# Down projections of a two-layer transformer kernel: eight of 22 combining sums a layer moved to accumulating DMA, LayerNorm rows behind the last weight halves

## The reference, cut to what matters

```python
def conv_ffn(x, w_up, conv_w, conv_b, w_down):
    up = x @ w_up
    a, g = up[..., :D_FF], up[..., D_FF:]
    g = causal_dwconv(g, conv_w) + conv_b
    return (jax.nn.gelu(g) * a) @ w_down

for layer in range(DEPTH):            # DEPTH = 2
    ...
    x = layer_norm(alpha * x + conv_ffn(x, ffn_w_up[layer], ffn_conv_w[layer],
                                        ffn_conv_b[layer], ffn_w_down[layer]),
                   ln_ffn_g[layer], ln_ffn_b[layer])
```

## Time and profile before

| | us |
|---|---|
| runs | 1760.81, 1761.2, 1763.09 |
| median | 1761.2 |
| the profiled execution's own time | 1760.65 |
| span of the profile | 1758.8 |
| TensorE busy / weight loads | 1728.8 / 1447.6 |
| VectorE, ScalarE, GpSimd busy | 1110.8, 684.7, 184.4 |

### The profile page before, as it was taken

The page is one execution under the profiler, slowest core; times in us unless marked ns, Lnnn a source line. Parts: engine busy times, 40 slices in busy tenths (PEclk is TensorE's granted clock), DMA queues, the critical chain, the costliest instruction groups (busy, mean ns, idle before and its releaser), DMA issues.

```text
span 1758.8 us, 27808 instructions
## 1 busy us (share of the span) xinstructions
PE 1728.8 (98%) x11461; PEld 1447.6 (82%) x11461; DVE 1110.8 (63%) x1624; ACT 684.7 (39%) x1045; POOL 184.4 (10%) x246
## 2 busy tenths in 40 slices
PE   8999999999999999999999999999998999999998
PEld 7888988988888879888998888888886767777766
DVE  5567266454568795454726755567988585566784
ACT  5332352232235643213235232223554543345452
POOL 4202001200011112000210200001112000011000
PEclk9999999999999999999999999999999999999999
DMA  9882912973345858833492265455683422112412
GB/s 301 259 217 99 252 39 79 279 230 110 126 138 186 260 166 204 247 97 118 114 283 77 83 204 156 143 183 185 201 277 108 153 65 81 34 43 62 169 37 84
DMA packets 175453, 270.44 MB, mean 154 GB/s; under 512 B 10488, under 2 KB 97780, under 8 KB 174560
## 3 DMA queue, kind: packets, MB, share of 16 engines
q1 hardware_dynamic: 147488, 189.90, 34.2%
q0 software_dynamic: 26368, 73.51, 15.7%
q10 hardware_dynamic: 1472, 5.26, 0.8%
HBM read 253.67 MB, written 61.09 MB: 179 GB/s over the span
## 4 chain that ended last, share of the span: by engine, by line
PE 88%; DVE 7%; issue 2%; ACT 1%; DMA 1%; POOL 1%; SPq 0%; ACTq 0%; DVEq 0%
PE ps L365 26%; PE ps L367 26%; PE ps L366 26%; DVE WL L342 2%; PE ps L1007 2%; PE ps L554 1%; PE ps L2575 1%; PE ps L2595 1%; PE ps L2589 1%; DMA RAW<-ffn_w_down 1%; PE ps L1981 0%; DVE SM L1637 0%; PE ps L2609 0%; DVE LATE L2656 0%; PE ps L2712 0%
## 5 line engine op out<-in xcount | busy, mean ns | idle before, releaser
L342 DVE TENSOR_TENSOR WL<-RAW,WH 128x1024 fp32r<-128x1024 f32 x325 | 393.3, 1222 | 387.7 <-ACT WH L332 387.2
L332 ACT ACTIVATE WH<-RAW 128x1024 fp32r<-128x1024 f32 x325 | 341.0, 1058 | 559.8 <-PE ps L367 450.6
L365 PE MATMUL ps<-XH,WH 128*128 128x512 f32 (+1 forms) x1416 | 524.6, 370 | 2.6 <-DVE WL L342 1.5
L367 PE MATMUL ps<-XH,WL 128*128 128x512 f32 (+1 forms) x1416 | 518.1, 366 | 0.0
L366 PE MATMUL ps<-XL,WH 128*128 128x512 f32 (+1 forms) x1416 | 517.9, 366 | 0.0
L365 PEld LDWEIGHTS ps<-XH,WH 128*128 128x128 f32 x1416 | 267.4, 189 | 50.1 <-issue 5.3
L367 PEld LDWEIGHTS ps<-XH,WL 128*128 128x128 f32 x1416 | 267.3, 189 | 43.3
L366 PEld LDWEIGHTS ps<-XL,WH 128*128 128x128 f32 x1416 | 267.5, 189 | 40.7
L365 PE MATMUL ps<-WH,XH 128*128 128x512 f32 x696 | 279.1, 401 | 7.9 <-DVE WL L342 7.0
L367 PE MATMUL ps<-WH,XL 128*128 128x512 f32 x696 | 271.9, 391 | 0.0
L366 PE MATMUL ps<-WL,XH 128*128 128x512 f32 x696 | 271.6, 390 | 0.0
(11 more groups left out here) (404 smaller groups left out, 2063.7 us busy)
## 6 DMA issues: line engine op xcount, KB each, us to landing
RAW<-ffn_w_up SPq DMA_DIRECT2D x176, 256.0 KB, 3.5
weight_sums<-ffn_w_down POOLq DMA_DIRECT2D x12, 1536.0 KB, 18.5
RAW<-w_in SPq DMA_DIRECT2D x33, 512.0 KB, 3.9
RAW<-xa_wkv SPq DMA_DIRECT2D x32, 512.0 KB, 7.5
RAW<-weight_sums SPq DMA_DIRECT2D x32, 512.0 KB, 4.6
weight_sums<-ffn_w_down POOLq DMA_DIRECT2D x12, 1280.0 KB, 31.1
RAW<-c_w_in SPq DMA_DIRECT2D x24, 512.0 KB, 7.2
LATE<-w_ada SPq DMA_DIRECT2D x24, 512.0 KB, 5.2
```

The source lines that it names most:

```text
L332: e.activation(halves_of(i)[0][:, :, 0:w], raw(i)[:, :, 0:w], ACT.Copy).then_inc(*w_hi.up(i))
L342: e.tensor_tensor(wl[:, :, 0:w], raw(i)[:, :, 0:w], wh[:, :, 0:w].bitcast(F), ALU.subtract).then_inc(*w_lo.up(i))
L365: e.matmul(o, lh, rh, start=start, stop=False)
L367: return e.matmul(o, ll, rh, start=False, stop=stop)
```

## The change

- ScalarE multiplies the residual by alpha in place, one row tile after each of the column blocks 2 to 5 of the up projection (`residual_act`).
- Eight of the 22 combining instructions become accumulating transfers that GpSimd issues (`combined_pool`): XR's blocks += U (rows 0, 1, column block 0), += the sum of U and product 6 (rows 2, 3, block 0), += Y (all rows, block 1). The sum no longer overwrites U but has its own place (`sum_place`). The adds and subtractions of product 7 move to steps 26 and 27; VectorE waits there, at step 28 and in rows 0 and 1 for the transfers.
- LayerNorm rows 0 and 1 move from steps 30 to 33 to behind the low half of chunk 39, ahead of rows 2 and 3; `row` is split in `row` and `row_g`, and the parts of neighbouring rows are interleaved.
- On TensorE, in layer 0, `behind(0)` moves from behind the last chunk of u = 0 to behind the second of the four chunks of u = 1, where `behind(1)` was, and `behind(1)` to behind all of e.
- On GpSimd `combined_pool` stands behind `down_pool`, ahead of `early_pool` and the LayerNorm steps.

```diff
@@ -316,6 +316,7 @@
     sum_in = {name: [sig(f"sum_{name}{g}", "dma", 16) for g in range(2)] for name in ("t1", "t2", "t3", "t4")}
     tok_out, tok_in = sig("tok_out", "dma", 16), [sig(f"tok_in{i}", "dma", 16) for i in range(3)]
     dn_a = sig("dn_a", "A")
+    comb = {name: sig(f"comb_{name}", "dma", 16) for name in ("x11", "x12", "x21", "x22")}
 
     made = {"hi": 0, "lo": 0, "w": 0}
 
@@ -1270,6 +1271,8 @@
             for i in range(2):
                 gate_act(e, l, nb, i)
                 gelu_act(e, l, nb, i)
+            if 2 <= nb < 6:
+                residual_act(e, l, turned, nb - 2)
         hi_to(e, first["up", l, 10] + 3 + NH)
         for i in range(2):
             gate_act(e, l, 10, i)
@@ -1277,6 +1280,11 @@
         hi_to(e, first["up", l, 10] + 4 + NH)
         gelu_act(e, l, 10, 0)
         gelu_act(e, l, 10, 1)
+
+    def residual_act(e, l, turned, t):
+        for q in range(2):
+            e.wait_ge(*turn.at((turned, t, q)))
+        e.activation(XR[:, t, :], XR[:, t, :], ACT.Copy, scale=ALPHA).then_inc(*ffn_a.up(("residual", l, t)))
 
     def gate_act(e, l, nb, i):
         j, key = 2 * nb + i, (("up", l, nb), 2 + i)
@@ -1351,6 +1359,27 @@
     U = [SCR[:, 1028 + 512 * u:1540 + 512 * u] for u in range(2)]
     Y = [SCR[:, 512 * u:512 * u + 512] for u in range(2)]
 
+    def sum_place(l, u):
+        return late(512 + 512 * u, 512) if l == 0 else late(4096 + 1024 * u, 512)
+
+    def combined_pool(e, l):
+        n = ("ffn", l)
+
+        def added(name, t, j, src):
+            e.wait_ge(*ffn_a.at(("residual", l, t)))
+            e.dma_start(XR[:, t, 512 * j:512 * j + 512], src, accum_op=ALU.add).then_inc(*comb[name].up((l, t)))
+        for u in range(2):
+            e.wait_ge(*dn_a.at(("u", l, u)))
+            added("x11", u, 0, U[u])
+        for u in range(2):
+            e.wait_ge(*ln_v.at((n, "sum", u)))
+            added("x21", 2 + u, 0, sum_place(l, u))
+        for u in range(2):
+            e.wait_ge(*ln_v.at((n, "y", u)))
+            added("x12", u, 1, Y[u])
+        for u in range(2):
+            added("x22", 2 + u, 1, Y[u])
+
     def token_place(l):
         return (late(1536, 512), late(2816, 256)) if l == 0 else (late(5120, 512), late(5632, 256))
 
@@ -1583,8 +1612,9 @@
             for u in range(2):
                 for q in range(2, 6):
                     part(name, q, u)
-                    if name == "e" and (u, q) in ((0, 5), (1, 3)):
-                        behind(u)
+                    if name == "e" and (u, q) == (1, 3):
+                        behind(0)
+        behind(1)
         ps.back(*[("down", l, p, u) for p in (3, 4) for u in range(2)])
 
     def items_at(s):
@@ -1636,9 +1666,6 @@
         def stats_of(t, j):
             e.bn_stats(stats[:, t, j, :], x(t, j)).then_inc(*ln_v.up((n, t, j, "stats")))
 
-        def scaled(t, j, src):
-            return e.scalar_tensor_tensor(out=x(t, j), in0=x(t, j), scalar=ALPHA, in1=src, op0=ALU.mult, op1=ALU.add)
-
         def add(p, t, j):
             key = ("down", l, p, t % 2)
             e.tensor_tensor(x(t, j), x(t, j), ps.tile(key)[:, :], ALU.add).then_inc(*ps.empties(key, ln_v, (n, t, j)))
@@ -1648,7 +1675,7 @@
             u = t % 2
             if t < 2:
                 e.wait_ge(*gemm.at(("down", l, 3, u)))
-                e.wait_ge(*ln_v.at((n, "x12", u)))
+                e.wait_ge(*comb["x12"].at((l, 1)))
                 add(3, t, 1)
                 stats_of(t, 1)
             else:
@@ -1656,6 +1683,8 @@
                 e.wait_ge(*ln_v.at((n, "x21", u)))
                 add(4, t, 0)
                 stats_of(t, 0)
+
+        def row_g(t):
             norm_g_dve(e, XR[:, t, :], n, t, 2, GB[:, 0:1024], gb_in.at(n))
 
         def row_end(t):
@@ -1665,49 +1694,35 @@
             item_lo(e, l, m)
         for s in range(34):
             for u in range(2):
-                if s == 20:
+                if s == 21:
                     e.wait_ge(*dn_a.at(("u", l, u)))
-                    scaled(u, 0, U[u]).then_inc(*ln_v.up((n, "x11", u)))
-                if s == 21:
                     e.wait_ge(*gemm.at(("down", l, 6, u)))
-                    e.wait_ge(*ln_v.at((n, "x11", u)))
-                    e.tensor_tensor(U[u], U[u], ps.tile(("down", l, 6, u))[:, :], ALU.add).then_inc(
+                    if l:
+                        e.wait_ge(*tok_out.at((l, 10)))
+                    e.tensor_tensor(sum_place(l, u), U[u], ps.tile(("down", l, 6, u))[:, :], ALU.add).then_inc(
                         *ps.empties(("down", l, 6, u), ln_v, (n, "sum", u)))
                 if s == 22:
                     e.wait_ge(*ln_v.at((n, "sum", u)))
                     e.wait_ge(*gemm.at(("down", l, 5, u)))
-                    e.tensor_tensor(Y[u], ps.tile(("down", l, 5, u))[:, :], U[u], ALU.subtract).then_inc(
+                    e.tensor_tensor(Y[u], ps.tile(("down", l, 5, u))[:, :], sum_place(l, u), ALU.subtract).then_inc(
                         *ps.empties(("down", l, 5, u), ln_v, (n, "y", u)))
-                if s == 23:
-                    e.wait_ge(*ln_v.at((n, "y", u)))
-                    scaled(u, 1, Y[u]).then_inc(*ln_v.up((n, "x12", u)))
-                if s == 24:
+                if s == 26:
                     e.wait_ge(*gemm.at(("down", l, 7, u)))
-                    scaled(2 + u, 0, ps.tile(("down", l, 7, u))[:, :]).then_inc(*ln_v.up((n, "ax21", u)))
-                if s == 25:
-                    scaled(2 + u, 1, Y[u]).then_inc(*ln_v.up((n, "ax22", u)))
-                if s == 26:
-                    e.wait_ge(*ln_v.at((n, "ax22", u)))
+                    e.wait_ge(*comb["x21"].at((l, 3)))
+                    e.tensor_tensor(x(2 + u, 0), x(2 + u, 0), ps.tile(("down", l, 7, u))[:, :], ALU.add).then_inc(
+                        *ln_v.up((n, "x21", u)))
+                if s == 27:
+                    e.wait_ge(*comb["x22"].at((l, 3)))
                     e.tensor_tensor(x(2 + u, 1), x(2 + u, 1), ps.tile(("down", l, 7, u))[:, :], ALU.subtract).then_inc(
                         *ps.empties(("down", l, 7, u), ln_v, (n, "x22", u)))
-                if s == 27:
-                    e.wait_ge(*ln_v.at((n, "ax21", u)))
-                    e.tensor_tensor(x(2 + u, 0), x(2 + u, 0), U[u], ALU.add).then_inc(*ln_v.up((n, "x21", u)))
                 if s == 28:
                     e.wait_ge(*gemm.at(("down", l, 2, u)))
+                    e.wait_ge(*comb["x11"].at((l, 1)))
                     add(2, u, 0)
                     stats_of(u, 0)
                 if s == 29:
                     e.wait_ge(*ln_v.at((n, "x22", u)))
                     stats_of(2 + u, 1)
-            if s == 30:
-                row(0)
-            if s == 31:
-                row_end(0)
-            if s == 32:
-                row(1)
-            if s == 33:
-                row_end(1)
             lo_to(e, min(i0 + s + 1 + NH, limit))
             if s == 1:
                 token_sums(e, l, 9)
@@ -1715,27 +1730,37 @@
                 token_sums(e, l, 10)
             for m in items_at(s):
                 item_lo(e, l, m)
+        lo_to(e, i0 + 35 + NH)
         if l:
-            lo_to(e, n_in2)
             e.wait_ge(*ada_v.at(("mod", 5)))
             e.scalar_tensor_tensor(out=s1, in0=mod[:, 8:16], scalar=1.0, in1=VEC[:, vcol["ng"]:vcol["ng"] + 8],
                                    op0=ALU.add, op1=ALU.mult).then_inc(*rms_v.up("s1"))
-            for t in range(2, 4):
+            for t in range(4):
                 row(t)
-                if t == 3:
-                    bias_dve(e, 2)
-                row_end(t)
+                if t:
+                    row_end(t - 1)
+                row_g(t)
+            bias_dve(e, 2)
+            row_end(3)
             bias_dve(e, 3)
             e.wait_ge(*rms_g.at(3))
             lo_to(e, n_in2 + 1)
             return
+        row(0)
+        row_g(0)
         lo_to(e, i0 + 36 + NH)
+        row_end(0)
+        row(1)
+        row_g(1)
         turn_dve(e, n, 0)
+        row_end(1)
         row(2)
+        row_g(2)
         turn_dve(e, n, 1)
         lo_to(e, i0 + 37 + NH)
         row_end(2)
         row(3)
+        row_g(3)
         lo_to(e, i0 + 38 + NH)
         row_end(3)
         lo_to(e, i0 + 39 + NH)
@@ -3122,6 +3147,7 @@
                         sums_pool(e, 1, 0)
                     tokens_pool(e, l)
                     down_pool(e, l)
+                    combined_pool(e, l)
                 if (name, l) == ("ffn", 1):
                     early_pool(e)
                 for t in range(4):
```

## The result

| | before | after |
|---|---|---|
| median (19 runs each) | 1761.73 us | 1766.1 us |
| lowest to highest | 1760.03 to 1765.18 | 1764.17 to 1769.8 |
| the profiled execution's own time / span | 1760.65 / 1758.8 | 1765.43 / 1763.4 |

The ratio is 1.0026, 95% interval 1.0019 to 1.0032: slower by a little more than the 0.2% that a measurement of this kernel can tell from no change. The forecast was 1764.0 in a range of 1757.5 to 1767.0. The time lies in it, 2.1 us above the forecast. The growth of 4.4 us is more than the 3.5 us that the prediction had called the same: that outcome had 0.62 there, and slower 0.25. The span grew by 4.6 us, where the sum had said 2.8. The question of this part is where the other 1.8 us are, and whether the terms of the sum are what the chip does or only happen to add up.

What follows compares the result with a forecast made beforehand. TensorE, busy 98% of the span, was taken as the bound. From a profiled 1760.65 us, +1.0 - 0.2 + 2.0 = +2.8 gives 1763.45; with the median 0.55 above it, 1764.0 us, range 1757.5 to 1767.

Steps and rivals of the forecast that it cites:

- The stalls: Four TensorE waits for low weight halves ending both down projections, 5.95 us, all go; gross gain 7.4 us.
- Layer 0, +1.0: At the next gemm's second chunk after layer 0, TensorE arrives 1.0 us later than before (0.3 to 2.0).
- the count: VectorE's work in layer 0 up to the next gemm's second chunk: 27.6 us, with waits 29.1, low half ready at 671.65.
- The three waits: In layer 0 TensorE waits at row 1's turn and the next gemm's first and second chunks, about 4.1 us.
- Layer 1, -0.2: Row 3's end in layer 1 starts at 1359.8 against 1359.96: -0.2 us (-0.8 to +1.0).
- Links: Steps from one row end to the next in layer 1, over VectorE, ScalarE and GpSimd: 4.6 us each, 5.0 before.
- The sign that was given: What would show the prediction right in layer 1: row 3's end within 1 us of 1359.96.
- The pause and the clock, +2.0: TensorE stands 4.9 us before layer 1's fifth transpose; the lower clock slows later transposes: +2.0 us (0 to 3.5).
- Rival B: Waits moved as forecast but TensorE's clock held through layer 1's pause: 1762.0 us, chance 0.25.
- What was costed at nothing: ScalarE's four scalings a layer and the eight transfers GpSimd issues cost nothing; the last transfer has 16 us of cover.
- Rival D: Accumulating transfers land late, VectorE waits at steps 26 and 27; 10 us beyond cover in one layer gives 1774, chance 0.07.
- Rival C: The removed stalls pay: layer 0 keeps 3.1 us and layer 1 some 3, giving 1755.1 us, chance 0.13.

Runs made afterwards that it cites:

- Rows alone: Experiment 2: kernel before with all 22 combining instructions, only the change's places of LayerNorm rows 0 and 1 and their turns, no transfers: 1764.4 us, ratio 1.0011.
- experiment 3: Changed kernel with the early transfers for the second block held until chunk 34 of layer 1's down projection instead of chunk 3: 1765.06 us, ratio 1.0012.
- experiment 4: Changed kernel with 40 more transposes, results unused, after row 0's fourth, filling TensorE's pause: 1765.3 us, ratio 1.0018.
- experiment 5: Rows alone with row 0's add, statistics and (x - mean) * g back at step 30, its end behind the last low half: 1761.65 us, ratio 1.0001.
- experiment 1: Changed kernel with rows 0 and 1 back at steps 30 to 33 and TensorE's turns at their old places: 1767.02 us, ratio 1.003.
- experiment 9: Experiment 5 with TensorE's turn of row 0 back after the sixth part of block e, as before the change: 1759.16 us, ratio 0.9976.
- experiment 8: Experiment 1 with the early transfers of the next stage held until chunk 34 instead of chunk 3: 1768.47 us, ratio 1.0042.

## Why the prediction was right, and what it missed

- **The stalls.** All four went; TensorE's first new wait is behind block e. Right.
- **Layer 0, +1.0.** Rows alone gave +1.19, +1.04 without the offset, with c1's low half ending 0.1 us from the 671.65 that the count gave (670.64 and 1.14 for it). The three waits were 3.2 us in all, where 4.1 were foretold. Right in place and size. The changed kernel has +1.88. Without the offset the three kernels with the change's own layer 0 (after, experiments 3 and 4) have 1.66, 1.51 and 1.17, so 0.1 to 0.6 us are the transfers'.
- **Layer 1, -0.2.** Links of 4.58 to 4.60 us, foretold 4.6; rows alone -0.25. Right for the rows. The sign that was given, row 3's end within 1 us of 1359.96, holds with the rows alone (1360.90) and fails in the changed kernel (1363.46).
- **The pause and the clock, +2.0.** The pause was 4.92 us (foretold 4.9), and experiment 4 shows that the lower clock is the cost. With the rows alone and in experiment 3 it cost 2.00 and 2.04 us, in the changed kernel 1.17: there the clock fell 1.8 us before the transposes and not with them, and 50 of them took 8.38 us against 9.20. When the clock falls within a pause is open. As a term of the sum for this execution it was 0.8 too large. Rival B, which had the clock held, is out. The rule of the Trainium skill that the prediction named (TensorE: Matmul & The Clock Gate, section Why this matters for your kernels), that such a pause between bursts of matmuls brings the lower clock back, held for the pauses of 4.5 to 5.0 us. The clock fell behind shorter ones too: 2.73 us in experiment 5 (0.57 in 1360 to 1364) and 1.89 us in experiment 1 (0.57 in 1337 to 1341), while it stayed up through 2.23 us in the kernel before and 2.33 in experiment 1's layer 0. So the length of a pause alone does not tell.
- **What was costed at nothing: the step that failed.** The prediction asked whether each transfer lands before VectorE needs its result (16 us of cover, which held: the last landed 11.9 and 12.4 us after its issue) and not whom it delays. Its price was near: 22 us for eight, 2.8 each, where the eight took 20. But 20 us of transfers in a stretch where the DMA engines were already busy 0.56 leave them no time (0.99), the loads got 143 GB/s where they had 167, and block d's weights were late: in layer 1 +1.62 us where -0.25 is what the rows alone give, in layer 0 0.1 to 0.6. The sentence that SyncE's loads only start earlier was wrong in its word "only", and the one that lines 1766 to 1771 come 8 us later and are needed long after left out that they come on top of the loads. Rival D priced late transfers at 10 us in one layer; the mechanism that came is its neighbour, at about 2. The scalings on ScalarE, also put at nothing, cost nothing that shows: ahead of the transfers the traces with and without them agree within the offsets (614.40 and 614.74 against 614.52 and 614.67).
- **The total.** +1.19 - 0.25 + 2.00 = 2.9 for the rows alone; the changed kernel has 0.69 and 1.87 more at the first two points and 0.83 less at the third, together the 4.67. The forecast was near because the rows' half was counted right. It was 1.8 us low because the transfers' half was not free, and would have been 2.6 us low without the luck that the clock term came out 0.8 smaller.
- **Rival C** (the stalls pay) fell for the reason given. But the reason pointed further than I took it: row 0's 2.88 us in VectorE's idle time were the thing to keep, and experiment 9, which keeps them, is 0.14 to 0.33% faster than the kernel before.

## What to carry to other kernels

Work that an engine does while it would wait anyway is free; moving it out to cure a stall behind it costs most of its length later (here 2.3 of row 0's 2.9 us in layer 0, by experiments 2 and 9 without their offsets). Move only what stands between the free slot and the stall, and look at every engine that has an order of its own for the same work: here the place of the turn on TensorE made the difference between no gain and 0.24% (experiments 5 and 9). A DMA that replaces an instruction is costed twice, for its own landing and for the loads that run beside it: read the DMA share of that stretch first, and ask which loads have no slack. And times from two traces are compared only after a look at a point ahead of the change: here it had moved by up to 1.3 us.

## What the runs showed of the hardware that was not expected

- Eight accumulating transfers of 256 KB within SBUF take 20 us together, each landing 5.3 to 12.4 us after its issue (median 7.3). The issue on GpSimd takes 0.85 to 1.9 us, and the eight raise the DMA share from 0.56 to 0.99.
- A one-element step on GpSimd took 0.22 or 1.31 us by what VectorE did beside it.
- Equal pauses of TensorE (4.92 and 4.95 us) cost 1.17 and 2.00 us of slower matmuls, by how much of the time at the lower clock lay inside the pause (1.8 and 0.2 us).
- A pause of 1.89 us was followed by the lower clock (experiment 1), pauses of 2.23 and 2.33 us were not.
- A one-element step on GpSimd stands behind DMA issues that are held: 4.36 us of waiting on VectorE (experiment 8).
